# Expert adds moved ahead of the next pair's products, last matrices loaded in quarters, and a ninth ring slot in layer two

## The reference, cut to what matters

```
def expert_choice_moe(h, w_router, w_gate, w_up, w_down):
    cap = EC_FACTOR * n // N_EXPERTS                  # 32 tokens for each of 16 experts
    aff = softmax(h @ w_router)
    g, idx = top_k(swapaxes(aff, 1, 2), cap)
    xs = h[idx]
    hid = silu(xs @ w_gate[e]) * (xs @ w_up[e])       # 1024 -> 512
    y = (hid @ w_down[e]) * g                         # 512 -> 1024
    return zeros.at[idx].add(y)
```

## Time and profile before

| | |
|---|---|
| median of 3 runs | 2781.36 us |
| profiled execution | 2785.59 us |
| its span | 2783.8 us |
| TensorE busy | 2581.8 us, 93% |
| VectorE busy | 1687.9 us, 61% |
| ScalarE busy | 904.0 us, 32% |
| bytes by DMA | 528.11 MB, mean 190 GB/s |

### The profile page before, as it was taken

One profiled execution on the slowest core, in us unless ns is written; L12 is line 12 of the kernel. 1 busy time (PEld: TensorE's weight loads), 2 busy tenths in 40 slices (PEclk: granted clock), 3 DMA queues, 4 the chain that ended last, 5 costly groups with the idle time before them and its releaser, 6 DMA issues. The chain is left out here.

```text
span 2783.8 us, 38292 instructions
## 1 busy us (share of the span) xinstructions
PE 2581.8 (93%) x14442; PEld 1895.3 (68%) x14442; DVE 1687.9 (61%) x2549; ACT 904.0 (32%) x1496; POOL 221.6 (8%) x372
## 2 busy tenths in 40 slices
PE   5999999998999999999999878998998999888987
PEld 4888887666887888887888658996566433565322
DVE  4876785444787778878678558786534232663101
ACT  2222225444422222522224444445333100543100
POOL 0010011221001101001110000000001000001000
PEclk9999998999999999999999999998999999999998
DMA  8666562332366756457664207664105899516998
GB/s 282 195 195 178 165 185 73 71 79 59 104 184 195 241 165 205 130 170 234 194 197 111 67 26 211 190 201 127 55 15 219 341 428 427 158 40 284 421 427 340
DMA packets 428866, 528.11 MB, mean 190 GB/s; under 512 B 29766, under 2 KB 382532, under 8 KB 416292
## 3 DMA queue, kind: packets, MB, share of 16 engines
q1 hardware_dynamic: 392592, 399.52, 41.8%
q0 software_dynamic: 35520, 126.24, 14.6%
q10 hardware_dynamic: 596, 0.19, 0.0%
HBM read 524.85 MB, written 1.05 MB: 189 GB/s over the span
## 5 line engine op out<-in xcount | busy, mean ns | idle before, releaser
L2165 DVE TENSOR_TENSOR wlo<-raw,whi 128x1024 fp32r<-128x1024 f32 x392 | 476.3, 1223 | 181.3 <-ACT whi L1607 170.0
L1607 ACT ACTIVATE whi<-raw 128x1024 fp32r<-128x1024 f32 x392 | 412.5, 1056 | 498.1 <-PE bank L709 449.5
L707 PE MATMUL bank<-xhi,whi 128*128 128x512 f32 (+1 forms) x1528 | 556.0, 364 | 0.0
L708 PE MATMUL bank<-xlo,whi 128*128 128x512 f32 (+1 forms) x1528 | 549.5, 360 | 0.0
L709 PE MATMUL bank<-xhi,wlo 128*128 128x512 f32 (+1 forms) x1528 | 549.2, 359 | 0.0
L2204 DVE SCALAR_TENSOR_TENSOR acc<-mod_ring,conds,acc 128x1024 f32<-128x1024 f32 x336 | 416.1, 1280 | 10.8 <-DMA mod_ring<-in_w_ada 4.5
L707 PEld LDWEIGHTS bank<-xhi,whi 128*128 128x128 f32 x1528 | 288.6, 189 | 57.4 <-issue 15.7
L709 PEld LDWEIGHTS bank<-xhi,wlo 128*128 128x128 f32 x1528 | 288.6, 189 | 43.8
L708 PEld LDWEIGHTS bank<-xlo,whi 128*128 128x128 f32 x1528 | 288.7, 189 | 41.5
L707 PE MATMUL bank<-hhi,whi 128*128 128x512 f32 (+1 forms) x764 | 269.3, 353 | 0.0
L709 PE MATMUL bank<-hhi,wlo 128*128 128x512 f32 (+1 forms) x764 | 266.5, 349 | 0.0
(11 more groups left out here) (346 smaller groups left out, 3536.6 us busy)
## 6 DMA issues: line engine op xcount, KB each, us to landing
raw<-in_ffn_w_in SPq DMA_DIRECT2D x176, 512.0 KB, 4.7
mod_ring<-in_w_mod POOLq DMA_DIRECT2D x128, 512.0 KB, 4.6
experts<-in_w_gate SPq DMA_DIRECT2D x32, 2048.0 KB, 20.7
experts<-in_w_up SPq DMA_DIRECT2D x32, 2048.0 KB, 20.1
experts<-in_w_down SPq DMA_DIRECT2D x32, 2048.0 KB, 21.1
mod_ring<-in_w_ada POOLq DMA_DIRECT2D x96, 512.0 KB, 4.9
raw<-in_ffn_w_out SPq DMA_DIRECT2D x64, 384.0 KB, 3.9
raw<-in_ffn_w_out SPq DMA_DIRECT2D x64, 320.0 KB, 3.3
```

The costliest lines, as they stand in the source:

```text
L707: pe.matmul(o, wh, hi[:, k0 + k, cols], start=(first and k == 0), stop=False)
L708: pe.matmul(o, wh, lo[:, k0 + k, cols], start=False, stop=False)
L1607: act.activation(whi[:, slot, :], raw[:, slot, :], ACT.Copy).then_inc(*n.mark("hi_ready"))
L2165: dve.tensor_tensor(wlo[:, slot, :], raw[:, slot, :], whi[:, slot, :].bitcast(F32), ALU.subtract)\
```

## The change

Three edits, all in the mixtures of experts.

1. In both layers `combine(p - 1, ...)` stands ahead of `gate_up(p, i)`, on TensorE, and the adds to `h` stand ahead of the multiplication for the hidden values on VectorE.
2. In both layers three units of pair 7 (up of both experts and the second down) are loaded by four DMAs of 512 KB each instead of one of 2 MB, each with its own semaphore, and the products wait for the quarter that they read.
3. In layer two the ring has a ninth slot, number 8, at the place of `h`. SP waits for `h_free`, which TensorE counts at the end of `residual_rows()`, before it loads the first unit into it. That unit is u = 8.

```diff
-RING_SLOTS = ((5, 6, 0, 1, 2, 3, 4), (7, 5, 6, 0, 1, 2, 3, 4))
+RING_SLOTS = ((5, 6, 0, 1, 2, 3, 4), (7, 5, 6, 0, 1, 2, 3, 4, 8))
...
-    experts = [at(f"experts{r}", [P, EXPERT_UNIT], F32, o) for r, o in enumerate([ring_at + 16 * KB * r for r in range(5)] + [big + 48 * KB, big + 32 * KB, big + 16 * KB])]
+    experts = [at(f"experts{r}", [P, EXPERT_UNIT], F32, o) for r, o in enumerate([ring_at + 16 * KB * r for r in range(5)] + [big + 48 * KB, big + 32 * KB, big + 16 * KB, base])]
...
+        def in_pieces(u):
+
+            kind, i = PAIR_UNITS[u % len(PAIR_UNITS)]
+            return u // len(PAIR_UNITS) == PAIRS - 1 and (kind == "up" or (kind, i) == ("down", 1))
+
+        def piece_full(l, name, j):
+
+            return s[f"piece_full{name[0]}{name[1]}_{j}"], 16 * (l + 1)
...
                     elif slot == 1:
                         sp.wait_ge(s["units_done"], RING + issued)
+                    elif slot == 8:
+                        sp.wait_ge(s["h_free"], 1)
...
+                    if in_pieces(u):
+                        for j in range(4):
+                            part = slice(j * D, (j + 1) * D)
+                            sp.dma_start(experts[slot][:, part], src[:, part]).then_inc(s[f"piece_full{kind}{i}_{j}"], 16)
+                        continue
                     sp.dma_start(experts[slot][:, :], src).then_inc(s[f"expert_full{slot}"], 16)
...
                     for j in range(KD):
+                        if p == PAIRS - 1 and j % 2 == 0:
+                            pe.wait_ge(*piece_full(l, ("up", i), j // 2))
...
                     for j in range(4):
+                        if p == PAIRS - 1:
+                            pe.wait_ge(*piece_full(l, ("down", 1), j))
...
-                                pe.matmul(bank[4 + 2 * half + t][:, j * P:(j + 1) * P], h[:, 4 * half + j, t * P:(t + 1) * P], tab("ident"),
-                                          start=(j == 0), stop=False, skip_group_check=True)
+                                mm = pe.matmul(bank[4 + 2 * half + t][:, j * P:(j + 1) * P], h[:, 4 * half + j, t * P:(t + 1) * P], tab("ident"),
+                                               start=(j == 0), stop=False, skip_group_check=True)
+                    mm.then_inc(s["h_free"], 1)
...
                 for p in range(PAIRS):
                     for i in range(2):
-                        gate_up(p, i)
                         if p:
                             combine(p - 1, (2 * i, 2 * i + 1))
+                        gate_up(p, i)
...
                 for p in range(PAIRS):
                     for i in range(2):
+                        if p:
+                            combined((2 * i, 2 * i + 1))
                         dve.wait_ge(*n.next("silu_ready"))
                         dve.wait_ge(*n.next("up_used"))
...
                         dve.sem_inc(*n.mark("hid_ready"))
-                        if p:
-                            combined((2 * i, 2 * i + 1))
```

More of the change, by code:

```diff
@@ L232 @@
     + [f"down_used{t}" for t in range(4)]
+    + [f"piece_full{u}_{j}" for u in ("up0", "up1", "down1") for j in range(4)]
+    + ["h_free"]
     + [f"st_done{g}" for g in range(2)]
@@ L483, in expert_full @@
             if l and slot in RING_SLOTS[0]:
-                earlier = len(range(RING_SLOTS[0].index(slot), LAYER_UNITS, len(RING_SLOTS[0])))
+                earlier = sum(not in_pieces(v) for v in range(RING_SLOTS[0].index(slot), LAYER_UNITS, len(RING_SLOTS[0])))
             return s[f"expert_full{slot}"], 16 * (earlier + u // len(RING_SLOTS[l]) + 1)
@@ L1476, in gate_up @@
                     for kind in ("gate", "up"):
-                        pe.wait_ge(*expert_full(l, p, (kind, i)))
+                        if (p, kind) != (PAIRS - 1, "up"):
+                            pe.wait_ge(*expert_full(l, p, (kind, i)))
                         slots.append(expert_slot(l, p, (kind, i))[1])
                     for j in range(KD):
+                        if p == PAIRS - 1 and j % 2 == 0:
+                            pe.wait_ge(*piece_full(l, ("up", i), j // 2))
                         for g in range(groups if p + i == 0 else 0):
@@ L1502, in down @@
                     for i in range(2):
-                        pe.wait_ge(*expert_full(l, p, ("down", i)))
+                        if (p, i) != (PAIRS - 1, 1):
+                            pe.wait_ge(*expert_full(l, p, ("down", i)))
                         slots.append(expert_slot(l, p, ("down", i))[1])
                     for j in range(4):
+                        if p == PAIRS - 1:
+                            pe.wait_ge(*piece_full(l, ("down", 1), j))
                         for half in range(groups):
```

## The result

| | median | runs | ratio to before, 95% interval |
|---|---|---|---|
| before | 2781.41 us | 2779.95 to 2786.03 | |
| changed kernel | 2809.98 us | 2806.71 to 2813.01 | 1.0101 [1.0087, 1.0115] |

The change costs 28.6 us (2809.98 - 2781.41), where +20.7 had been forecast. To see where, I cut each profiled execution at four instants of TensorE: the start of layer one's first products, the end of its last down products, the start of layer two's first products, the end of its last down products. In the table (us), "middle" is what lies between the two mixtures, "rest" what follows the second. All kernels of the experiments stand in it, each with its one profiled execution.

What follows compares the result with a forecast made beforehand. Transfers were taken to bound both mixtures, TensorE only 3 us per pair faster in layer one. Layer one +9.2, layer two +10.5, clock +1.0 gave +20.7, so 2802 us against the 2781.36 median; range 2789 to 2815.

Steps and rivals of the forecast that it cites:

- The forecast case: Whole kernel: all terms as worked out, time 2802 us, within 2797 to 2807; chance 0.68.
- the first rival: TensorE's clock falls in most pairs, six falls or so: 10 us more than the 1 taken, 2812; chance 0.13.
- The two waits of layer one: TensorE, each pair: 1.21 us for the ysb copy, 1.75 at the turn; +9.2 us after eating 11.5 of waits.
- No wait for a transfer in layer one, first products 29.3 apart: Sign in layer one: pairs start 29.3 us apart, with no wait for a transfer behind pair 1.
- The clock: TensorE's clock falling after pauses: 1 us taken in all; ends 0 and 12 in layer one and 3 in layer two.
- The quarters in layer one: Pair 7's quarter loads in layer one give nothing: last unit lands at 2376.1, TensorE asks at about 2387.
- The ninth slot: Layer two: unit 8 issued 16.1 us later, units 9 to 12 behind it, last landing +14.9 us.
- The quarters in layer two: End of layer two: three of four down steps run before the last landing, -4.9 us; twelve quarters cost 0.5.
- hidden by them: Layer two: TensorE's pair grows by both waits but stays some 4 us below the transfers' 29.4, costing nothing.
- no wait was hidden: Answers two rivals on layer one's waits: partly hidden, 2792 us, chance 0.08; both hidden, 2786, chance 0.04.
- the slot did reach the transfers: Answers the rival that unit 8's wait never reaches the transfers: 2786 us, or 2771 with waits hidden; chance 0.05.
- the quarters paid next to nothing: Answers the rival that each quarter pays a fixed part in a full queue: 20 us in layer two, 2822; chance 0.02.

Runs made afterwards that it cites:

- filler: Changed kernel with two useless matmuls in TensorE's pause between the second products and the turn, against the changed kernel: 2801.24 us, ratio 1.0064 to the kernel before.
- adds_filler: Kernel before with all adds in front in both layers, plus two useless matmuls in the pause ahead of the turn: 2795.15 us, ratio 1.0054.
- adds_only: Kernel before with only the adds moved in front, in both layers, on TensorE and VectorE: 2799.91 us, ratio 1.0072.
- adds_quarters: Kernel before with the adds in front and the quarter loads, ring of eight slots kept: 2801.1 us, ratio 1.0073.
- slot_only: Kernel before with only the ninth ring slot in layer two: 2794.14 us, ratio 1.0047.
- quarters_only: Kernel before with only the quarter loads, in both layers: 2771.83 us, ratio 0.9951.
- slot_early: Kernel before with the ninth slot, and residual_rows() moved ahead of layer two's first products: 2776.64 us, ratio 0.9980.

## Why the prediction was right, and what was mis-sized

The direction held, and 2809.98 lies in the range, 8 us above the forecast. The forecast case, 2797 to 2807, was not quite the one that happened: 2809.98 is near the 2812 of the first rival, the clock falling in most pairs, on top of the forecast's own two waits.

- **The two waits of layer one: right.** 1.21 and 1.75 were forecast, 1.21 (1.14 by the row's count) and 1.62 measured. Their net cost, forecast at 9.2, is 8.4 in filler and adds_filler, the filler's own 1.5 us in pair 0 taken off; the missing 0.8 is about that of the second wait, 7 x 0.13.
- **No wait for a transfer in layer one, first products 29.3 apart: half right.** The waits are gone; the pairs are 30.8 apart, by the clock.
- **The clock: the mis-sized term.** I took 1 us in all. The seven slow downs of layer one sum to 60.6 us against 49.5: 11.1 us, near the upper end of 12 that I had named. The row I leaned on, products at full speed behind a single wait of 2.12 us, was not the situation to come: two pauses, 1.56 and 0.69 us, with only 0.75 us of transposes between. Filler shows that in layer one there is no fall without the longer of them. In the working this was a term between ends 0 and 12 for which I took a value near 0 by a row of another shape.
- **The quarters in layer one: right** (0 with the adds in front; adds_only to adds_quarters +2.2, of which 1.7 is one more fall of the clock). Alone they would have given 4.2.
- **The ninth slot: right.** The issue moved by 16.1 us, as forecast; the last landing by 15.5 (forecast 14.9 + 0.5), in slot_only by 15.1; slot_only costs 14.5 in the stage.
- **The quarters in layer two: right in size, with less to spare.** The tail fell from 5.8 to 1.6 us, 4.2 of 4.9 forecast. Down's steps did not wait for their quarters, because TensorE was late itself.
- **The growth of TensorE's pair in layer two "hidden by them": true only here.** My ground for it, a pair shorter than the transfers', was wrong: with the adds alone TensorE's pair stays shorter and still ends the layer, 5.2 us late, since it has to catch up with eight loaded units first. The right comparison is the one I made in layer one, seven increments against the reserve. With my own waits (7 x 2.96 = 20.7 against 27.1) it would have said hidden too; with the clock's 7 x 1.7 in it, not. In the changed kernel the slot's 15 us enlarge the reserve, so the growth is covered: layer two is +11.3, where 14.5 + 5.2 - 3.1 = +16.6 would be the sum of the edits alone. They don't add up; the later of two chains counts.
- **Sum:** layer one +19.6 (9.2, and the 1.0 for the clock, forecast), layer two +11.3 (10.5), middle +0.7, rest -1.5. The profiled execution took 2806.71 and thus looks like a hit on the 2806.3 worked out for it; that is chance, since the part ahead of the mixtures was 9.0 us shorter in it.
- **The other rivals:** no wait was hidden (both rows stand), the slot did reach the transfers, and the quarters paid next to nothing: 0.6 us for all twelve, 0.5 forecast. It takes 25.0 us from the landing of unit 42, the last one ahead of the quarters, to the last landing in the changed kernel, quarters_only and adds_quarters, and 24.4 to 24.5 us in before, adds_only and slot_only. The rate is 418 GB/s from 2770 to 2790, among the quarters, and 427 from 2630 to 2760, ahead of them. The Trainium skill ("DMA: Bandwidth & Descriptors", section Anatomy of one DMA — SWDGE (gpsimd) path) counts about 2 us fixed for each transfer on the path that it measured; behind a full queue this trace does not show them.

Open: the 3 us by which quarters_only's median is better than its stages, and what besides the pause decides whether the clock falls.

## What to carry to other kernels

Work that stands in a gap of another engine's chain is a cover, and two covers may stand in the same block of work: before it is moved, ask of each half what it covers. Count a pause of TensorE as time, and name what it may cost by the clock on top; here that was as much again (1.6 us of pause, 1.5 to 1.7 us of clock). Whether a longer step is hidden by transfers is read from the sum of waits that the layer has now, not from the comparison of two rates; and then the transfers are followed too, since a slower first pair can let them run dry. A further ring slot whose first use waits for a late reader makes an in-order queue stall for all the units behind it; free the place first, as slot_early does. To give the slot to a later unit would be the other way; it was not run.

## What the runs showed of the hardware

- In layer one TensorE's clock hung on a pause of 1.6 us: with the pause idle 8.6 to 8.8 us for 64 matmuls in 7 of 7 pairs (8.5 to 8.6 in 6 of 7 in adds_only) and a clock of 0.83 over 10 us, with useless matmuls in it 7.07 us in all pairs, and 9.6 us less in the layer. In layer two of the changed kernel the same pause was followed by a slow down in 3 of 7 pairs.
- The issue of a DMA itself can hold SP: the four quarters of the last down unit of layer two took 435 to 5761 ns each, 9.3 us together, where those of layer one took 328 to 432. How long the transfers ahead still ran did not decide it: the four quarters issued from 2740.3 on landed only after 31.4 to 33.7 us and took 328 to 427 ns. For an expert unit or a quarter it took over 2 us only in kernels with quarters, and there only while nine or more DMAs of SP were issued and not yet landed; the cause was not tested. It cost nothing here, as the pipe was full.
- The stretch before the mixtures, the same in all twelve kernels, took 2153.7 to 2163.6 us, so that single spans can't show effects under 10 us.
- Quarters of 512 KB in the place of 2 MB transfers behind a full queue cost 0.6 us for twelve (25.0 and 24.4 us for the last five units).
